# Selection of the dense PEER tokens spread over more blocks of a hybrid decoder step on one core

## The reference

```python
q = (xb @ w_q).reshape(blk, PEER_HEADS, 2, PEER_HALF)
s = jnp.einsum('thcd,hcnd->thcn', q, sub_keys)
s_top, i_top = lax.top_k(s, PEER_TOPK)                    # 16 of 128 keys, twice
cand_s = s_top[:, :, 0, :, None] + s_top[:, :, 1, None, :]  # 256 pairs
best_s, best_pos = lax.top_k(cand_s, PEER_TOPK)
expert = take_along_axis(cand_e, best_pos)                # 16 of 16384 experts a head
gate = softmax(best_s)
act = gelu(einsum('td,thkd->thk', xb, u[expert]))
y = einsum('thk,thkd->td', gate * act, v[expert])
```

## Time and profile before

| | |
|---|---|
| median of 3 runs | 5276.35 us (5275.28 to 5283.59) |
| profiled execution | 5254.98 us |
| span of its instructions | 5253.1 us |
| PE busy | 4308.1 us, 82% of the span |
| DVE busy | 3096.9 us, 59% |
| POOL busy | 1920.2 us, 37% |
| ACT busy | 1026.1 us, 20% |
| moved by DMA | 1099.26 MB, mean 209 GB/s |

### The profile page before, as it was taken

How to read it: one execution, slowest core, us unless ns; L and a number is a source line. 1 busy time by engine, 2 the same in 40 slices (tenths; PEclk the granted TensorE clock), 3 DMA queues, 4 the chain that set the end, 5 groups by cost and what they waited for, 6 DMA issues and landing times. The chain is left out here.

```text
span 5253.1 us, 56097 instructions
## 1 busy us (share of the span) xinstructions
PE 4308.1 (82%) x21158; PEld 3533.7 (67%) x21158; DVE 3096.9 (59%) x5685; ACT 1026.1 (20%) x2272; POOL 1920.2 (37%) x1559
## 2 busy tenths in 40 slices
PE   6989679788997559996787799996888997469995
PEld 5467438577886458885555688863677886458884
DVE  1315540599957796656216633345599867796656
ACT  0102310222332150000012222211222332150000
POOL 0000230166657624444002433312256557614444
PEclk9985669899998779998878788858899998779997
DMA  2330112488889948998111000013588889939998
GB/s 91 89 75 1 34 37 96 167 301 313 311 338 397 369 128 342 409 396 348 56 58 35 1 1 1 1 41 104 188 300 310 319 341 390 363 109 371 409 399 333
DMA packets 403487, 1099.26 MB, mean 209 GB/s; under 512 B 70508, under 2 KB 157261, under 8 KB 402886
## 3 DMA queue, kind: packets, MB, share of 16 engines
q0 software_dynamic: 186496, 679.04, 34.4%
q1 hardware_dynamic: 216726, 416.69, 22.6%
HBM read 1066.88 MB, written 32.45 MB: 209 GB/s over the span
## 5 line engine op out<-in xcount | busy, mean ns | idle before, releaser
L1036 DVE SCALAR_TENSOR_TENSOR gg_ytok<-gg_ring,gg_gw,gg_ytok 128x1024 f32<-128x1024 f32 x320 | 422.1, 1319 | 178.5 <-DMA gg_ring<-in_peer_v,gg_idx 172.5
L1036 DVE SCALAR_TENSOR_TENSOR fg_ytok<-fg_ring,fg_gw,fg_ytok 128x1024 f32<-128x1024 f32 x320 | 422.0, 1319 | 176.6 <-DMA fg_ring<-in_peer_v,fg_idx 170.0
L706 POOL DMA_INDIRECT fg_ring<-in_peer_u,fg_idx x320 | 377.2, 1179 | 351.7 <-DVE fg_ring L1030 284.4
L706 POOL DMA_INDIRECT gg_ring<-in_peer_u,gg_idx x320 | 374.4, 1170 | 345.7 <-DVE gg_ring L1030 275.9
L1030 DVE SCALAR_TENSOR_TENSOR fg_ring<-fg_ring,fg_htok 128x1024 f32<-128x1024 f32 x320 | 409.7, 1285 | 128.1 <-DMA fg_ring<-in_peer_u,fg_idx 126.4
L1030 DVE SCALAR_TENSOR_TENSOR gg_ring<-gg_ring,gg_htok 128x1024 f32<-128x1024 f32 x320 | 409.8, 1286 | 127.8 <-DMA gg_ring<-in_peer_u,gg_idx 125.7
L774 PE MATMUL fg_bank<-f_hTd,fg_uT 128*128 128x256 f32 x2048 | 476.9, 387 | 0.6 <-ACT f_buf L873 0.6
L774 PE MATMUL gg_bank<-g_hTd,gg_uT 128*128 128x256 f32 x2048 | 476.2, 387 | 0.6 <-ACT g_buf L873 0.6
L706 POOL DMA_INDIRECT gg_ring<-in_peer_v,gg_idx x320 | 358.1, 1119 | 272.1 <-DVE gg_ytok L1036 211.8
L706 POOL DMA_INDIRECT fg_ring<-in_peer_v,fg_idx x320 | 345.7, 1080 | 276.3 <-DVE fg_ytok L1036 214.4
L774 PEld LDWEIGHTS fg_bank<-f_hTd,fg_uT 128*128 128x128 f32 x2048 | 389.8, 196 | 51.2 <-issue 0.9
(11 more groups left out here) (620 smaller groups left out, 7758.8 us busy)
## 6 DMA issues: line engine op xcount, KB each, us to landing
fg_ub<-in_peer_u SPq DMA_DIRECT2D x128, 512.0 KB, 6.8
gg_ub<-in_peer_u SPq DMA_DIRECT2D x128, 512.0 KB, 6.7
fg_ub<-in_peer_v SPq DMA_DIRECT2D x64, 512.0 KB, 7.2
fg_uT<-in_peer_v SPq DMA_DIRECT2D x64, 512.0 KB, 6.7
gg_ub<-in_peer_v SPq DMA_DIRECT2D x64, 512.0 KB, 7.3
gg_uT<-in_peer_v SPq DMA_DIRECT2D x64, 512.0 KB, 6.8
f_buf<-in_peer_w_q SPq DMA_DIRECT2D x16, 1024.0 KB, 12.2
g_buf<-in_peer_w_q SPq DMA_DIRECT2D x16, 1024.0 KB, 11.8
```

Of the source, the lines that this page charges most:

```text
L706: pool.indirect_dma_start(ring[:, n % RING, :], None, (u_rows if kind == "u" else v_rows)[:, :], bass.IndirectOffsetOnAxis(ap=idx[:, r:r + ...
L1036: dve.scalar_tensor_tensor(ytok[:, :], row, gw[:, r:r + 1], ytok[:, :], ALU.mult, ALU.add).then_inc(used, 1)
```

## The change

`UNITS_SEL` gives the dense passes 55, 55, 55 and 30 gathered rows instead of 26 each (107 rows then follow the selection instead of 198), and `BLOCKS_SEL` gives them 18, 18, 18 and 14 blocks instead of 9 each, so that the selection reaches to block 97 instead of block 65. The buffers at the end of the large buffer are put into another order, and ACT's single wait at block 79 is split into five: block 79 (`lim_w`, for the last query), 95 (`lim_q`, last scores), 108 (`lim_s`, last first use of the scores), 113 (`lim_rest`, last subtraction of the best) and 118 (`lim_hit`, last indices). `HTR_AT` moves by 1024 columns, so `lim_a` is block 69. The gap for gelu in `place` is 40 instead of 25.

```diff
-UNITS_SEL = (0, 20, 24, 24, 26, 26, 26, 26)
-BLOCKS_SEL = (3, 8, 9, 9, 9, 9, 9, 9)
+UNITS_SEL = (0, 20, 24, 24, 55, 55, 55, 30)
+BLOCKS_SEL = (3, 8, 9, 9, 18, 18, 18, 14)
 UNITS_U = 370
-HTR_AT = 16640
+HTR_AT = 17664
...
+        hit = top_of_buf(10 * TOPK * TOPK).rearrange("p (a e i j) -> p a e i j", a=2, e=5, i=TOPK)
+        lim_hit = free[0] // TD
+        s_rest = top_of_buf(10 * P).rearrange("p (e c n) -> p e c n", e=5, c=2)
+        lim_rest = free[0] // TD
+        s_sb = top_of_buf(10 * P).rearrange("p (e c n) -> p e c n", e=5, c=2)
+        lim_s = free[0] // TD
+        qT = top_of_buf(4 * TR).rearrange("p (h c t) -> p h c t", h=2, c=2)
         keysT = top_of_buf(HC * P).rearrange("p (h n) -> p h n", n=P)
+        lim_q = free[0] // TD
         wt = top_of_buf(4 * D).rearrange("p (b k n) -> p b k n", b=2, k=KD)
-        qT = top_of_buf(4 * TR).rearrange("p (h c t) -> p h c t", h=2, c=2)
-        s_sb = top_of_buf(10 * P).rearrange("p (e c n) -> p e c n", e=5, c=2)
-        s_rest = top_of_buf(10 * P).rearrange("p (e c n) -> p e c n", e=5, c=2)
-        hit = top_of_buf(10 * TOPK * TOPK).rearrange("p (a e i j) -> p a e i j", a=2, e=5, i=TOPK)
-        lim_end = free[0] // TD
+        lim_w = free[0] // TD
         lim_a = HTR_AT // TD
...
-        for c, k in zip(early_chunks, place(sched, [dots_at[c] for c in early_chunks], 25.0)):
+        for c, k in zip(early_chunks, place(sched, [dots_at[c] for c in early_chunks], 40.0)):
...
-                        if b == lim_end:
-                            act.wait_ge(gate_done, npass)
+                        if b == lim_w:
+                            act.wait_ge(mm_done, 4 * npass)
+                        if b == lim_q:
+                            act.wait_ge(sc_done, npass)
+                        if b == lim_s:
+                            act.wait_ge(s_used, npass)
+                        if b == lim_rest:
+                            act.wait_ge(off_done, npass)
+                        if b == lim_hit:
                             act.wait_ge(idx_done, npass)
```

More of the change, by code:

```diff
@@ L563, in peer_layer @@
             if p + 1 < npass:
+                assert nb <= lim_w, (nb, lim_w)
                 some_queries(p + 1)
@@ L567, in peer_layer @@
                 assert nb <= lim_a, (nb, lim_a)
-        assert nb <= lim_end, (nb, lim_end)
         some_blocks(nblk - nb)
```

## The result

The changed kernel took 5238.24 us (median of 4 runs, 5228.81 to 5243.13) against 5277.24 us for the kernel before (4 runs); the ratio is 0.9928, 95% interval 0.9905 to 0.9951. It is faster, by 39 us. The forecast was 94 us and 5182 us: the direction held and the time lies within the stated range of 5120 to 5242, but the gain is 39 us and not 94.

The account below looks back on a forecast made before the run. DVE bounds the first half of the PEER window, DMA the second. DMA work of 563 to 581 us, taken as 577 instead of 624.3, saves 47 us in each of two layers, 94 in all: 5182 us, range 5120 to 5242.

Parts of the forecast that it names:

- What bounds the kernel: First PEER layer, 624.3 us window: DVE bounds the first half, DMA the second, with a 25 us hole between.
- The work that stays: DMA transfers left in that window: gathers 408, u blocks 132, query weights 16, plain copies 7, together 563 us.
- the other reading: The same window's DMA work taken as its share 0.93 of 624.3 us: 581 us.
- How full the engines are: Dense passes with 55 rows: six slots and u blocks keep DMA near 0.98; window 577 us, 47 less a layer.
- Rival C: Window's DMA share stays at 0.93 through bursts of 11 units and 8 us pauses; no change, 5276 us; chance 0.09.
- Scores and blocks: Dense passes under the new block counts: PE has scores ready before DVE asks, cover 40 us or more.
- The last exponential: ACT does it after block 97, at 1594 us, before DVE asks at 1612; the 22.75 us wait goes.
- Order of buffers and the gelu gap: ACT's five buffer limits cost nothing, cover 70 us; gap 25 to 40 ends PE earlier but is worth nothing itself.
- Rivals B and D: In the window, POOL's gather issue becomes the bound, 5446 us, chance 0.06; or PE starves for blocks, 5258 us, 0.07.
- The 358 GB/s a core: Skill's HBM load limit: the window's 217 MB would take 607 us, 17 less a layer, about 5242 in all.

Follow-up runs that it names:

- the fastest kernel: The changed kernel with seven ring slots, rows after every selection step, look-up product on DVE and the last exponential 34 planned us earlier: 5134.47 us, ratio 0.9730.
- the second experiment: The changed kernel with seven ring slots instead of six, candidate buffers moved into the large buffer: 5166.03 us, ratio 0.9788.

## Why the prediction was wrong, step by step

- **What bounds the kernel**: right. DVE bounded the dense passes, DMA what followed, and a hole of 25 us lay between. With the holes closed the stretch stands at a DMA share of 1.00 and no other engine above 0.89.
- **The work that stays**: right. 563 us at a full share were summed, or 581 by the other reading; the fastest kernel ran 563 us at 1.00, and the changed one 608 at 0.94, which is 571 of work. The work of a pass was summed as 108 us; measured it is 118.7 x 0.92 = 109, 117.4 x 0.94 = 110 and 116.3 x 0.91 = 106.
- **How full the engines are: the step that failed.** The text said that "six ring slots hold 6 x 1.35 = 8.1 us of transfers, and blocks of u come beside them, so the engines stay fed", and took a share near 0.98. It was 0.94, and 571 us of work at 0.94 are the 608 us measured. Three things in that step were wrong. Cover was compared with the pause of 8.3 us alone, but it has to last until the first row after the pause has been used, its slot issued (1.74 us at 1479.27) and its bytes flow, 12.2 us after the pause began. Six slots were counted as six gathers still to come: it was four, 2.13 MB or 5.3 us instead of 8.1 (2.0 to 2.2 MB in the seven other pauses of this kind in both layers). And the blocks of u were to fill what was left, but one comes only as fast as PE turns them: 1.33 us of transfer in a pitch of 4.33, an estimated share of 0.31. They brought 4.3 us, and some 2.5 stayed empty. That this was the error is shown from three sides: more slots (578 us), shorter pauses (596 and 591 us) and both (563 us) each gave back time with the same transfers. What one slot is worth was itself under-reckoned in the second experiment, 30 us a layer against 8 to 16. All of it lies in the three full dense passes, 322 us together instead of 352; the part after the last sums of hits took 186 us with seven slots and 185 with six.
- **Rival C** described what happened, "bursts of 11 units and pauses of 8 us" keeping the share low, and got 0.09. Its price was too high: at 0.94 instead of 0.93, and with work of 571 instead of 581 us, 16 and 13 us a layer were left.
- **Scores and blocks**: right, and more than a detail. DVE never waited for scores; with the old block counts ACT waited 67.9 us and nothing was gained.
- **The last exponential**: right for the change (22.75 us went; ACT waited for DVE instead). It is not safe: it returned with 27.9 us as soon as DVE got faster.
- **Order of buffers and the gelu gap**: costed at nothing. The gap alone gave 1.0006 and its return 0.9940, so right. The buffers could not be tried apart: with the old single wait, block 79 would wait for the selection while the last exponential stands behind block 96 in ACT's order. No wait at the five limits shows in the profile.
- **Rivals B and D**: neither happened. POOL's issues took 1.26 us (rows of u) and 1.16 (rows of v) on the mean of the passes; PE waited 24.7 us for blocks in the stretch (19.9 before), and ended at 1781, 60 us before DVE. PE's end was forecast 511 us after the stretch began and came after 548.
- **The 358 GB/s a core** did not bind: the fastest kernel moved 386 GB/s over 563 us. The Trainium skill ("DMA: Bandwidth & Descriptors", section "Bandwidth") also gives this figure as what each core gets when both cores of a pair stream; here one core ran.

## What to carry to other kernels

Work spread between transfers pays in full only if what is in flight outlasts the longest pause and the restart behind it. Sum pause, first use, issue and first bytes, and compare that with what is still to come when the pause begins; here that was four transfers of six slots. Where a slot more cannot be had, cut the pause. When an in-order plan on one engine is tuned to another's pace, a faster stage moves the wait to the next planned place, so look there before judging a combination by its total.

## What the runs showed that was not expected

One slot of six is worth more than its size: with 4, 6 and 7 slots the stretch took 723, 608 and 578 us in the first layer, and the DMA share was 0.85, 0.94 and 0.98. And in a stage that no kernel here changes, the same 25 us ran at a PE clock of 0.98 in one profiled execution and of 0.50 in another, and the first PEER layer began 18 us later in the second, more than the change gained in either layer.
